# Delta rule of a hybrid decoder step: row products moved from GpSimd to ScalarE and VectorE, queries and keys turned earlier, tile norms placed behind the new values

## The reference, cut to what matters

```python
gc = jnp.cumsum(g, -1)                      # within a chunk
decay = jnp.exp(where(lower_triangle, gc_i - gc_j, -inf))
k_beta = k * beta
A = strict_lower((k_beta @ k.T) * decay)
rhs = concat([v * beta, k_beta * jnp.exp(gc)])
u, w = split(triangular_solve(I + A, rhs))
qk = (q @ k.T) * decay
# scan over the chunks
v_new = u - w @ S
o = (q * exp(gc)) @ S + qk @ v_new
S = S * exp(g_last) + (k * exp(g_last - gc)).T @ v_new
# behind it
o = o * rsqrt(mean(o * o) + eps) * dn_norm_g * silu(z)
```

## Time and profile before

| | |
|---|---|
| three runs, us | 2219.65, 2220.26, 2227.92 (median 2220.26) |
| profiled execution, us | 2228.68; its span 2226.6 |
| busy over the span | PE 95%, PEld 86%, DVE 74%, ACT 35%, POOL 26% |
| delta phase | from 310.61 us to about 492.6 us of the span |

### The profile page before, as it was taken

One profiled execution on the slowest core, in us unless ns is written; L12 is line 12 of the kernel. 1 busy time (PEld: TensorE's weight loads), 2 busy tenths in 40 slices (PEclk: granted clock), 3 DMA queues, 4 the chain that ended last, 5 costly groups with the idle time before them and its releaser, 6 DMA issues. The chain is left out here.

```text
span 2226.6 us, 33908 instructions
## 1 busy us (share of the span) xinstructions
PE 2109.9 (95%) x12934; PEld 1910.4 (86%) x12934; DVE 1641.7 (74%) x3051; ACT 773.2 (35%) x1237; POOL 569.1 (26%) x354
## 2 busy tenths in 40 slices
PE   8997987979999989999999999999989999999998
PEld 7997877977965689999999999999987787778776
DVE  5634637666234332699999979999988888898898
ACT  4334332232233132222224434444443333333332
POOL 0000014000000000021211215555546655675530
PEclk9998778999999999999999999999999999999999
DMA  5223210023244040267765848989889999999993
GB/s 162 84 89 110 72 54 1 8 88 138 77 170 170 22 136 17 100 234 250 271 230 196 278 148 334 337 334 335 333 340 381 388 388 387 383 384 388 379 375 122
DMA packets 223216, 483.75 MB, mean 217 GB/s; under 512 B 12015, under 2 KB 137199, under 8 KB 221446
## 3 DMA queue, kind: packets, MB, share of 16 engines
q1 hardware_dynamic: 177030, 314.56, 39.8%
q0 software_dynamic: 46080, 167.79, 20.8%
HBM read 423.29 MB, written 58.36 MB: 216 GB/s over the span
## 5 line engine op out<-in xcount | busy, mean ns | idle before, releaser
L2873 PE MATMUL ps<-v_high_low,gated_high_low 128*128 128x512 f32 x2304 | 535.1, 393 | 22.6 <-ACT gated_high_low L2941 17.6
L2873 PEld LDWEIGHTS ps<-v_high_low,gated_high_low 128*128 128x128 f32 x2304 | 434.7, 190 | 122.8 <-ACT v_high_low L2939 20.6
L2477 PE MATMUL ps<-x_high_low,u_high_low 128*128 128x384 f32 x1024 | 355.6, 347 | 0.2 <-ACT u_high_low L2543 0.2
L2478 PE MATMUL ps<-x_high_low,u_high_low 128*128 128x384 f32 x1024 | 345.0, 337 | 0.0
L2965 POOL DMA_INDIRECT outputs<-peer_v,kept x138 | 256.7, 1860 | 170.4 <-DVE kept L2982 137.6
L2594 POOL DMA_INDIRECT scores<-peer_u,kept x64 | 94.1, 1470 | 781.6 <-DVE kept L2714 604.7
L2482 PE MATMUL ps<-x_high_low,u_high_low 128*128 128x384 f32 x1024 | 204.7, 341 | 0.0
L2552 ACT ACTIVATE kept<-ps 128x384 f32<-128x384 f32 x128 | 62.9, 491 | 406.4 <-PE ps L2482 400.0
L2477 PEld LDWEIGHTS ps<-x_high_low,u_high_low 128*128 128x128 f32 x1024 | 192.5, 188 | 0.5 <-ACT u_high_low L2543 0.5
L2478 PEld LDWEIGHTS ps<-x_high_low,u_high_low 128*128 128x128 f32 x1024 | 192.8, 188 | 0.0
L3045 DVE TENSOR_TENSOR v_high_low<-raw_v,v_high_low 128x1024 fp32r<-128x1024 f32 x120 | 146.4, 1220 | 52.9 <-ACT v_high_low L2939 52.9
(11 more groups left out here) (453 smaller groups left out, 4295.3 us busy)
## 6 DMA issues: line engine op xcount, KB each, us to landing
experts<-peer_u SPq DMA_DIRECT2D x63, 1024.0 KB
raw_v<-peer_v SPq DMA_DIRECT2D x60, 1024.0 KB
hidden<-kept SPq DMA_DIRECT2D x64, 384.0 KB
gates<-scores SPq DMA_DIRECT2D x12, 2048.0 KB
first_hidden<-hidden SPq DMA_DIRECT2D x16, 768.0 KB, 18.7
outputs<-gates SPq DMA_DIRECT2D x16, 768.0 KB
outputs<-hidden SPq DMA_DIRECT2D x16, 768.0 KB
first_gates<-gates SPq DMA_DIRECT2D x15, 768.0 KB
```

The costliest lines, as they stand in the source:

```text
L2477: pe.matmul(o, utr[:, b, HI, k], xr[:, HI, k, 0:DN], start=(k == 0), stop=False)
L2478: pe.matmul(o, utr[:, b, HI, k], xr[:, LO, k, 0:DN], start=False, stop=False)
L2873: ins = pe.matmul(bank(c, 2 * t + h), gr[:, slot, x, DN * b + P * t:DN * b + P * t + P], vr[:, slot, y, D * b + 512 * h:D * b + 512 * h + ...
```

## The change

GpSimd keeps only the mask and the subtraction of the level-0 inverse, which now wait for `at_set` alone. The decayed keys become eight ScalarE activations a tile (`decayed_keys`: identity function, with a scale per row), for tiles 0 to 3 in the front, one step behind the exponentials, and for tile 4 behind the sixth copy of the inverse. Beta times values becomes four such activations a tile (`beta_values`), behind the first five copies of the inverse. The gate gains become five VectorE products (`gate_gains`) behind updates 8 to 12.

TensorE turns queries and keys in a function of their own (`turn_qk`): for tile 0 behind the first sums, for tile n + 1 behind the products of tile n. `unit_length` now sets a semaphore (`unit_set`) instead of being waited for on the spot. ScalarE's copies of the turned rows wait in two parts. In the scan, `norm_tile(n - 1)` moves from the end of step n - 1 to behind the samples' new values of step n.

The diff, without its context lines, eight columns further left, and without the declarations of the two new semaphores and of `GAINS_AT = 8`:

```diff
@@ -1067,17 +1069,25 @@
+    def turn(n, sources):
+        r = ROWS[n]
+        for o, src in sources:
+            for h in range(DNH):
+                ins = pe.transpose(bank(c, o)[:, r * h:r * h + r], src[0:r, P * h:P * h + P], ident[0:r, 0:r])
+        return ins
+    def turn_qk(n):
+        pe.wait_ge(unit_set, n + 1)
+        turn(n, ((2, ct[:, n, 0:512]), (3, ct[:, n, 512:1024]))).then_inc(turned_qk, 1)
+    turn_qk(0)
-            pe.wait_ge(turned3_act, n)
-        for i, src in enumerate((ct[:, n, 0:512], ct[:, n, 512:1024], beta_k(n), qe)):
-            for h in range(DNH):
-                ins = pe.transpose(bank(c, 2 + i)[:, r * h:r * h + r], src[0:r, P * h:P * h + P], ident[0:r, 0:r])
-        ins.then_inc(turned3, 1)
+        turn(n, ((4, beta_k(n)), (5, qe))).then_inc(turned3, 1)
@@ -1089,6 +1099,8 @@
+        if n + 1 < NT:
+            turn_qk(n + 1)
@@ -1197,8 +1209,7 @@
-    spread_decay(0)
-    for n in range(NT):
+    def row_exps(n):
@@ -1209,12 +1220,41 @@
-        act.wait_ge(turned3, n + 1)
+    def keep_turned(n):
+        r = ROWS[n]
+        act.wait_ge(turned_qk, n + 1)
-        for i in range(3):
-            ins = act.copy(qkt[:, n % 2, i, 0:4 * r], bank(c, 2 + i, 4 * r))
-        ins.then_inc(turned3_act, 1)
+        for i in range(2):
+            act.copy(qkt[:, n % 2, i, 0:4 * r], bank(c, 2 + i, 4 * r))
+        act.wait_ge(turned3, n + 1)
+        act.copy(qkt[:, n % 2, 2, 0:4 * r], bank(c, 4, 4 * r)).then_inc(turned3_act, 1)
+    def decayed_keys(n):
+        r = ROWS[n]
+        act.wait_ge(exps, n + 1)
+        for h in range(DNH):
+            act.activation(ct[0:r, n, P * h:P * h + P], beta_k(n)[0:r, P * h:P * h + P], ACT.Identity, scale=eg[0:r, n, h:h + 1])
+        for h in range(DNH):
+            x = ct[0:r, n, 512 + P * h:640 + P * h]
+            ins = act.activation(x, x, ACT.Identity, scale=eg[0:r, n, 4 + h:5 + h])
+        ins.then_inc(kg_set, 1)
+    def beta_values(n):
+        r = ROWS[n]
+        for h in range(DNH):
+            x = ct[0:r, n, 1024 + P * h:1152 + P * h]
+            ins = act.activation(x, x, ACT.Identity, scale=beta[0:r, n, h:h + 1])
+        return ins
+    spread_decay(0)
+    row_exps(0)
+    for n in range(NT):
+        keep_turned(n)
+        if n + 1 < NT:
+            row_exps(n + 1)
+            decayed_keys(n)
@@ -1223,6 +1263,12 @@
+        if i == NT:
+            decayed_keys(NT - 1)
+        elif i < NT - 1:
+            beta_values(i)
+        elif i == NT - 1:
+            beta_values(i).then_inc(bv_set, 1)
@@ -1281,6 +1327,7 @@
+        v.wait_ge(unit_set, n + 1)
@@ -1289,10 +1336,10 @@
-    step(unit_length(0))
+    unit_length(0).then_inc(unit_set, 1)
-    step(unit_length(1))
+    unit_length(1).then_inc(unit_set, 1)
@@ -1304,7 +1351,7 @@
-            step(unit_length(n + 2))
+            unit_length(n + 2).then_inc(unit_set, 1)
@@ -1314,7 +1361,7 @@
-    v.wait_ge(kg_set, NT)
+    v.wait_ge(kg_set, NT - 1)
@@ -1331,6 +1378,13 @@
+    def gate_gains(n):
+        r = ROWS[n]
+        z = hd[0:r, n, 8:520].rearrange("p (h k) -> p h k", h=4)
+        if n == 0:
+            v.wait_ge(gain_in, 16)
+        v.tensor_tensor(z, z, over(ng[0:r], 1, [r, 4, P]), ALU.mult).then_inc(gain_set, 1)
@@ -1338,6 +1392,8 @@
+        if GAINS_AT <= i < GAINS_AT + NT:
+            gate_gains(i - GAINS_AT)
@@ -1359,7 +1415,7 @@
-    v.wait_ge(gain_set, 1)
+    v.wait_ge(gain_set, NT)
@@ -1380,6 +1436,7 @@
+            norm_tile(n - 1)
@@ -1395,39 +1452,18 @@
-            norm_tile(n)
-    def rows(n, a, scale, k, src=None):
-        r = ROWS[n]
-        o = ct[0:r, n, a:a + 512].rearrange("p (h k) -> p h k", h=4)
-        return pool.tensor_tensor(o, o if src is None else src, over(scale[0:r, n, k:k + 4], 2, [r, 4, P]), ALU.mult)
-        pool.wait_ge(prepared, n + 1)
-        pool.wait_ge(turned3, n + 1)
-        rows(n, 0, eg, 0, beta_k(n)[0:r].rearrange("p (h k) -> p h k", h=4))
-        rows(n, 512, eg, 4).then_inc(kg_set, 1)
-    for n in range(NT):
-        ins = rows(n, 1024, beta, 0)
-    ins.then_inc(bv_set, 1)
-    pool.wait_ge(gain_in, 16)
-    for n in range(NT):
-        r = ROWS[n]
-        z = hd[0:r, n, 8:520].rearrange("p (h k) -> p h k", h=4)
-        ins = pool.tensor_tensor(z, z, over(ng[0:r], 1, [r, 4, P]), ALU.mult)
-    ins.then_inc(gain_set, 1)
```

More of the change, by code:

```diff
@@ L1027, in phase_delta @@
     w_o0, c.w_oh0 = words(c, M_G, 2, D), rounded(c, "w_o_high0", M_WOH, 2, D)
-    gain_set, bv_set, kg_set = (s("delta_" + x) for x in ("gate_gains_set", "beta_v_set", "decayed_k_set"))
+    gain_set, bv_set, kg_set, unit_set, turned_qk = (s("delta_" + x) for x in (
+        "gate_gains_set", "beta_v_set", "decayed_k_set", "unit_rows_set", "q_and_k_turned"))
+    GAINS_AT = 8
     items = [(lev, n) for lev in range(1, LEVELS) for n in range(NT) if n < 4 or lev < 2]
```

## The result

Five runs of the changed kernel took 2198.21 to 2208.07 us, median 2202.68; five of the kernel before, the three above among them, 2219.65 to 2227.92, median 2227.36. The ratio is 0.9912, with a 95% interval of 0.9892 to 0.9932: faster by 0.7 to 1.1%.

A forecast was written before the change was run, and what follows sets the result against it. The phase's longest path was taken as the bound: front, stall, TensorE-bound inverse, scan. Gains 5.7 + 9.6 + 4.6 = 19.9 us off the 2220.26 median gave 2200.4 us, range 2194 to 2211 (8 in 10).

The forecast's parts named there:

- The stall: Start of the inverse: GpSimd's queued row products hold a VectorE mask; moving them away gains 9.6 us, bounds 7.2 and 10.4.
- The rival of another cause: Something other than GpSimd holds the long mask at the inverse's start, so only 10.3 us are gained; chance 0.08.
- The front ring: Loop of turns, sums, VectorE's differences and row products over four tile steps: 27.8 instead of 33.46 us, 5.7 gained.
- the first step: First of the front's four tile steps, at the lower clock: 1.84 turns, 2.3 sums, 3.45 the rest, 7.6 us.
- Who bounds the ring: In the front, ScalarE's loop of 6.1 us was to exceed the 5.8 path, VectorE's 5.75 and TensorE's 5.35.
- 0.7 of contention: In steps two to four of the front, GpSimd's level-0 masks hold VectorE's small copy: 0.7 us each, bounds nothing and 1.27.
- ScalarE's price for the keys: In the front, eight scaling activations a tile for the decayed keys, 0.29 us start to start: 2.35 us.
- The rival falls for this kernel: ScalarE becomes the bound of the front, by dearer activations or table reloads: 14.7 or 12.3 us gained; chance 0.13.
- Tables: In the front, still one function-table load; identity beside exponentials forces no reload on ScalarE.
- Work put into the inverse: Norm gains on VectorE, beta values and tile 4's decayed keys on ScalarE cost nothing under TensorE; 3.0 us if gains uncovered.
- The scan: Norm moved behind the next tile's new values takes 1.5 us off TensorE's wait in three tiles: 4.6 us, bounds 0 and 5.3.
- The rival that goes the other way: The lower clock stays through the inverse: all gains gone after nine items, 2250 us over all 25; chance 0.03.

The follow-up runs named there:

- both experiments on GpSimd's queue: Kernel before, once with beta values on ScalarE and norm gains on VectorE (phase 174.40 us), once with GpSimd's ten row products held until the ninth item (182.10 us).
- the edit's own experiment: Kernel before with beta values on ScalarE and norm gains on VectorE, decayed keys left on GpSimd: phase 174.40 us, 9.85 less.
- GpSimd's products later: Kernel before with GpSimd's ten row products held back until the ninth item of the inverse: phase 182.10 us, 2.15 less.
- late turns: Changed kernel with queries and keys turned again together with the decayed rows: phase 170.49 us, 7.7 more.
- keys on VectorE: Changed kernel with decayed keys as two VectorE products a tile instead of eight ScalarE activations: phase 166.82 us, 4.1 more.
- keys on GpSimd: Changed kernel with only the decayed keys put back on GpSimd: phase 167.16 us, 4.4 more.
- tile 4's mask: Changed kernel with small rows read from PSUM and tile 4's triangle mask made a step earlier: phase 164.51 us, six runs with ratio 0.9895.

## Why the prediction was right, point by point

The time, 2200.4 us, stood 2.3 under the measured median. It was counted from a median of before of 2220.26; from the later 2227.36 it would have been 2207.5. So the gain is the better measure: summed 19.9, measured 21.5 in the phase, and by whole times 0.0088 of 2227.36, 19.6 (interval 15 to 24). That these lie so close is in part luck: front, stall and scan gave 1.9, 0.8 and 0.5 us more than summed, and a fall of the clock that was not summed took 1.6 back. Step by step:

- **The stall.** Right in cause: both experiments on GpSimd's queue show it. The gain is 10.4 against 9.6; I had kept 4.7 us, and the stretch took the 3.9 that I gave as its bound. That 3.9 came in the five traces in which the granted clock was 1.00 there. In the five others without the stall the clock was 0.66 to 0.90, and the stretch took 4.3 to 5.75 (4.67 in the edit's own experiment): the last 0.8 us are the clock's. The rival of another cause falls.
- **The front ring.** The structure was right and the size short by 1.9 us. The term at fault is the first step, summed as 7.6 at the lower clock: it took 5.86, since the clock rose during it. In six of the seven traces with early turns the clock was up within about 6 us of the phase's start, and in none of the five without; in the seventh the step took 8.00, near the sum. So 1.7 us of the front's gain are the clock's, and not in every run. Steps two to four were summed as 6.8, 6.8, 6.6 and took 6.61, 6.61, 6.74.
- **Who bounds the ring.** I named ScalarE, at 6.1, with 0.7 of contention on top. That was misread: of the 2.18 us for exponentials and spreading, 0.73 were waiting for VectorE, as this line of before shows.

```profile
324.37 0.63 ACT L1209 ACTIVATE layer<-layer 128x512 f32<-128x512 f32 x1 [0.73 <-DVE layer L1278]
```

Without it ScalarE's loop is 5.4, and 5.2 was measured. And the contention is on VectorE's copy, which lies on the ring and not in ScalarE's loop. So the prediction's own figures give 5.8 + 0.7 = 6.5 for the ring against 6.61 measured, and 5.75 + 0.7 = 6.45 for VectorE's loop against 6.35; that the summed 6.8 came near is luck. ScalarE's price for the keys was right (2.34 against 2.35), and it has slack. The rival falls for this kernel; one copy more, and it comes true for a step.

- **Tables.** One load in the front, so no reload between exponential and identity. The Trainium skill, page "ScalarE: Activation LUTs", section "Table sets: the hidden batching unit", had it so, and the trace agrees.
- **Work put into the inverse.** Summed as nothing; it cost 0.5 us, since three of the five items with a gain are 0.16 longer. Over the whole stretch only 0.1 of this shows, as the first item took 2.68 instead of 3.03. Of the slack of 0.79, 0.2 or 0.36 is left behind a gain.
- **The scan.** 4.6 summed, 4.6 measured by itself. A further 0.4 behind the last tile comes with the gains and beta values (there too in their own experiment) and was not followed up.
- **The clock.** The rival that goes the other way did not come: 1.00 over the inverse. But the clock took back 1.6 us between u and w and the scan. This shows in seven traces (the changed kernel twice, GpSimd's products later, late turns, keys on VectorE, keys on GpSimd, and tile 4's mask) and in five not (11.9 against 10.3 us). In five of the seven the clock had been 1.00 from the first product to the first update, and in none of the other five; but two of the seven (0.83 and 0.66 there) don't fit. I found nothing in the edits that parts these two groups; it stays open.

## What to carry to other kernels

Before an engine is relieved, list the idle time of all engines within one step of the loop: work goes to the one that has slack, even at nearly twice the price for the work (ScalarE 2.34 us for nothing, VectorE 1.2 us for 4.1 in the end). GpSimd work that nobody needs yet is not free: keep it out of stretches where VectorE has short two-input work on SBUF on the path. And where the runs of a kernel spread by more than the change, compare the length of the changed phase in the traces, and take out what its clock did.

## What the runs showed of the hardware, unexpected

A VectorE instruction that meets GpSimd isn't stretched in proportion: it can be held through several of GpSimd's instructions. One of 0.68 us took 9.59 beside a queue of ten products, 5.53 beside the last five of them, and 0.94 to 1.52 beside others; one of 0.15 on four columns took 1.24. With an input from PSUM in its place, the four-column copy took 0.16 beside the same masks.

TensorE's granted clock fell to 0.57 in a stretch in which it was busy 4.00 of 4.00 us. And with the same instructions in the first step, the clock was 1.00 from 6 to 12 us behind the phase's start in one kernel and 0.50 in another.
